# Bias rows sent out head by head beside the second mixer, constants loaded in two parts, and the first mixer's output projection done with split weights

## What is computed

```
def first_block(x, ...):
    ...
    for layer in range(DEPTH):                      # layer 0: even_mixer, layer 1: diff_mixer
        u = rms_norm(h, mix_norm_g[layer])
        h = h + mixer(u, ...)
        h = h + sq_relu_mlp(rms_norm(h, mlp_norm_g[layer]), mlp_w_up[layer], mlp_w_down[layer])
    return rms_norm(h, final_norm_g)
def even_mixer(h, w_in, cmp_pe, cmp_w1, cmp_w2, w_out, cos, sin):
    proj = jnp.einsum('btd,de->bte', h, w_in)
    ...
    o_a = dsa_attention(qa, ka, va, qi, ki, wi)     # 8 heads, top-k of an index score
    o_b = nsa_attention(qb, k_c, v_c, k_s, v_s, k_w, v_w, gb, cmp_pe, cmp_w1, cmp_w2)   # 8 heads
    o = jnp.concatenate([o_a.reshape(bsz, T, -1), o_b.reshape(bsz, T, -1)], axis=-1)
    return jnp.einsum('bte,ed->btd', o, w_out)
def moba_attention(h, w_qkv, w_o, rel_bias):        # the last mixer
    ...
        bias_own = rb[t5_bucket(jnp.maximum(dist_own, 0))].transpose(2, 0, 1)[None]
        logit_own = jnp.einsum('bhqd,bhkd->bhqk', qf, k_own.astype(jnp.float32)) * scale + bias_own
```

## Time and profile before

| | us |
|---|---|
| median of three runs (1263.09 to 1263.97) | 1263.24 |
| the profiled execution, as timed | 1265.12 |
| its span in the trace | 1263.2 |
| PE busy in the span | 1155.1 (91%) |
| DVE busy | 807.2 (64%) |
| ACT busy | 592.3 (47%) |

### The profile page before, as it was taken

How to read it: one execution, slowest core, us unless ns; L and a number is a source line. 1 busy time by engine, 2 the same in 40 slices (tenths; PEclk the granted TensorE clock), 3 DMA queues, 4 the chain that set the end, 5 groups by cost and what they waited for, 6 DMA issues and landing times.

```text
span 1263.2 us, 18055 instructions
## 1 busy us (share of the span) xinstructions
PE 1155.1 (91%) x7384; PEld 1015.3 (80%) x7384; DVE 807.2 (64%) x1287; ACT 592.3 (47%) x914; POOL 45.7 (4%) x88
## 2 busy tenths in 40 slices
PE   4169999999999999899999849999999998999997
PEld 4167675999998877699999649999978987999996
DVE  4035734787777666787777686877775556655554
ACT  5023534634445556564344545444446454644342
POOL 1010000000000000000000000000002000000000
PEclk9679999999999999999999969999999999999999
DMA  7852403797773433569777334977735434455530
GB/s 267 122 138 71 167 27 149 297 354 276 272 293 134 167 104 130 200 254 351 276 273 277 119 133 155 359 276 279 298 134 180 154 133 150 168 199 180 187 134 34
DMA packets 35810, 248.57 MB, mean 197 GB/s; under 512 B 4304, under 2 KB 4320, under 8 KB 6928
## 3 DMA queue, kind: packets, MB, share of 16 engines
q1 hardware_dynamic: 26352, 188.61, 40.3%
q0 software_dynamic: 9232, 57.69, 13.8%
q10 hardware_dynamic: 144, 1.12, 0.2%
HBM read 242.55 MB, written 4.19 MB: 195 GB/s over the span
## 4 chain that ended last, share of the span: by engine, by line
PE 80%; DVE 9%; ACT 4%; issue 4%; DMA 3%; POOL 0%; DVEq 0%; ACTq 0%; POOLq 0%
PE bank L1216 67%; DMA bias_rows<-PT 3%; PE bank L1398 2%; PE bank L1632 2%; PE bank L1423 1%; DVE wlo L700 1%; PE bank L1615 1%; ACT vo L426 1%; DVE x L720 1%; DVE wlo L811 1%; PE bank L1447 1%; PE bank L1446 1%; PE bank L1445 1%; DVE work L718 1%; PE bank L1696 1%
## 5 line engine op out<-in xcount | busy, mean ns | idle before, releaser
L700 DVE TENSOR_TENSOR wlo<-raw,whi 128x2048 fp32r<-128x2048 f32 (+2 forms) x143 | 324.6, 2274 | 138.0 <-ACT whi L416 137.9
L1216 PE MATMUL bank<-uh,whi 128*128 128x256 f32 x1272 | 369.6, 291 | 36.4 <-ACT vo L522 36.4
L1216 PE MATMUL bank<-ul,whi 128*128 128x256 f32 x1272 | 361.4, 284 | 0.0
L1216 PE MATMUL bank<-uh,wlo 128*128 128x256 f32 x1272 | 361.4, 284 | 0.0
L416 ACT ACTIVATE whi<-raw 128x2048 fp32r<-128x2048 f32 (+2 forms) x143 | 270.5, 1896 | 38.9 <-DMA bias_rows<-PT 37.8
L1216 PEld LDWEIGHTS bank<-uh,whi 128*128 128x128 f32 x1272 | 245.4, 193 | 44.8 <-issue 42.5
L1216 PEld LDWEIGHTS bank<-ul,whi 128*128 128x128 f32 x1272 | 245.5, 193 | 4.4 <-issue 2.2
L1216 PEld LDWEIGHTS bank<-uh,wlo 128*128 128x128 f32 x1272 | 245.2, 193 | 0.0
L1216 PE MATMUL bank<-whi,hh 128*128 128x512 f32 x544 | 214.0, 393 | 0.0
L1216 PE MATMUL bank<-wlo,hh 128*128 128x512 f32 x544 | 212.4, 390 | 0.0
L1216 PE MATMUL bank<-whi,hl 128*128 128x512 f32 x544 | 211.8, 389 | 0.0
(11 more groups left out here) (211 smaller groups left out, 1185.7 us busy)
## 6 DMA issues: line engine op xcount, KB each, us to landing
raw<-in_stream SPq DMA_DIRECT2D x176, 1024.0 KB, 4.9
qk<-in_w_mod POOLq DMA_DIRECT2D x48, 1024.0 KB, 5.9
bias_rows<-PT POOLq DMA_DIRECT2D x1, 3072.0 KB, 33.0
u<-bias_rows POOLq DMA_DIRECT2D x16, 128.0 KB, 2.7
raw<-in_stream SPq DMA_DIRECT2D x2, 696.0 KB, 12.5
con<-in_con ACTq DMA_DIRECT2D x1, 1098.5 KB, 6.9
x<-in_x SPq DMA_DIRECT2D x2, 512.0 KB, 8.1
vo<-in_fin_g POOLq DMA_DIRECT2D x2, 512.0 KB, 4.9
```

The costliest lines, as they stand in the source:

```text
L700: nc.vector.tensor_tensor(wlo[:, c % RING, 0:w], raw[:, raw_index(c) % RING, 0:w], whi[:, c % RING, 0:w].bitcast(fp32), ALU.subtract).then ...
L1216: ins = mm(out, st, mv, start=start and i == 0, stop=stop and i == 2, skip_group_check=True)
```

## The change

**Bias rows.** `gb` gets a buffer of its own, 16 by 384. ACT no longer waits for `bias_out`. POOL writes the rows in 16 DMAs, one for each head and so from one partition each, and head h waits until chunk h - 1 of DIFF is used. **Constants.** They are reordered: 337 columns that the start needs go first, on SP's queue behind the first half of x; the other 1860 go behind stream chunk 1, and DVE waits for them (`in_late`) ahead of the lower part of chunk 4. **Start.** ACT takes a square root of a constant before x is there, splits chunk 0 ahead of the gain of the first token tile and chunk 1 behind it, and DVE follows. **Projection back.** The four output chunks are split like the others (they get numbers 10 to 13, and MLP0 begins at 14). ACT writes the upper part of each attention output quarter and DVE the lower part, into `hh`/`hl` and `uh`/`ul`; PE uses `add_rows` (L1216 of before), three passes in place of one float32 product.

```
@@ sync @@
             for t in range(NT):
                 sp.dma_start(x[:, t, :], a["x"][128 * t:128 * t + 128, :]).then_inc(in_x[t], 16)
+                if t == 0:
+                    sp.dma_start(con[:, 0:C_EARLY], a["con"][:, 0:C_EARLY]).then_inc(in_con, 16)
             for n in range(NRAW):
+                if n == 2:
+                    sp.dma_start(con[:, C_EARLY:], a["con"][:, C_EARLY:]).then_inc(in_late, 16)
@@ gpsimd @@
-            pool.wait_ge(bias_sb, 1)
-            pool.dma_start(bass.AP(gdram.tensor, 0, [[128 * 512, 16], [512, 128], [1, 384]]),
-                           gb[:, :].unsqueeze(1).to_broadcast([16, 128, 384])).then_inc(bias_out, 16)
...
+                elif m == 1:
+                    for h in range(16):
+                        pool.wait_ge(used, DIFF + h)
+                        pool.dma_start(bass.AP(gdram.tensor, 128 * 512 * h, [[512, 1], [512, 128], [1, 384]]),
+                                       gb[h:h + 1, :].unsqueeze(1).to_broadcast([1, 128, 384])).then_inc(bias_out, 16)
@@ scalar @@
-            act.dma_start(con[:, :], a["con"]).then_inc(in_con, 16)
+            act.wait_ge(col_ready, 1)
+            nc.scalar.activation(std[:, 0:1], one, ACT.Sqrt)
             deviation(0)
-            hi_upto(1)
             act.wait_ge(in_con, 16)
             for t in range(NT):
+                hi_upto(t)
                 upper(0, t, vec[:, V_MIX:])
...
-            act.wait_ge(bias_out, 16)
...
-                    nc.scalar.activation(oT[c], bank[7 if c else 6][:, :].rearrange("p (b n) -> p b n", b=2), ACT.Copy)\
-                        .then_inc(e_oc, 1)
+                    nc.scalar.activation(out_part(c, True), bank[7 if c else 6][:, :].rearrange("p (b n) -> p b n", b=2), ACT.Copy)\
+                        .then_inc(e_oh, 1)
...
-                elif (i, q) in ((16, 0), (17, 0)):
-                    hi_upto(MLP0 + i - 16)
+                elif (i, q) in ((12, 3), (13, 2), (14, 2), (15, 1), (16, 1), (17, 1)):
+                    hi_upto(i - 2)
@@ vector @@
-            dve.wait_ge(in_con, 16)
             for t in range(NT):
                 scaled(0, t)
+            dve.wait_ge(in_con, 16)
...
-                elif (i, q) in ((16, 3), (17, 2)):
-                    lo_upto(MLP0 + i - 16)
+                elif (i, q) in ((13, 3), (14, 1), (14, 3), (15, 3), (16, 3), (17, 2)):
+                    lo_upto({(13, 3): 10, (14, 1): 11, (14, 3): 12, (15, 3): 13, (16, 3): 14, (17, 2): 15}[i, q])
+                if (i, q) in E_TURN_OUT:
+                    c = E_TURN_OUT[i, q]
+                    dve.wait_ge(e_oh, c + 1)
+                    nc.vector.tensor_tensor(out_part(c, False), bank[7 if c else 6][:, :].rearrange("p (b n) -> p b n", b=2),
+                                            out_part(c, True).bitcast(fp32), ALU.subtract).then_inc(e_ol, 1)
@@ tensor @@
                     if p in (8, 10):
-                        pe.wait_ge(e_oc, p // 2 - 2)
+                        pe.wait_ge(e_ol, p // 2 - 2)
...
-                even_back(c, even_steps(E_OUT + c))
+                pe.wait_ge(lo_ready, MLP0 - 4 + c + 1)
+                pe.wait_ge(e_ol, c + 1)
+                add_rows(MLP0 - 4 + c, 1, out_part(c, True), out_part(c, False), c == 0, c == 3, steps=steps)
```

More of the change, by code:

```diff
@@ L21 @@
 LAM_INIT = 0.8 - 0.6 * math.exp(-0.3)
-C_ID, C_SW, C_TRI = 0, 128, 256
-C_COS, C_SIN, C_COSQ, C_SINQ = 384, 640, 896, 1152
-C_CORR = 1408
+C_ID, C_VEC = 0, 128
+V_MIX, V_MLP, V_MIX2, V_MLP2, V_POOL, V_C, V_SUB = 0, 16, 32, 48, 64, 72, 80
+V_BMOD = 81
+V_PE = V_BMOD + 96
+C_EARLY = C_VEC + V_PE + 32
+C_SW = C_EARLY
+C_TRI = C_SW + 128
+C_COS, C_SIN, C_COSQ, C_SINQ = (C_TRI + 128 + 256 * i for i in range(4))
+C_CORR = C_SINQ + 256
 C_HB = C_CORR + 128
@@ L30 @@
 C_MASK = C_CMPN + NT * NBLK
-C_VEC = C_MASK + 384
-V_MIX, V_MLP, V_MIX2, V_MLP2, V_POOL, V_C, V_SUB = 0, 16, 32, 48, 64, 72, 80
-V_BMOD = 81
-V_PE = V_BMOD + 96
-C_END = C_VEC + V_PE + 32
+C_END = C_MASK + 384
 QA, QI, KA, KI, QB, KC, VC, KS, KW = 0, 4, 6, 7, 8, 12, 13, 14, 15
-EVEN, MLP0, DIFF, MLP1, POOL, MLP2, MOBA, MLP3, LAST = 0, 10, 42, 58, 90, 91, 123, 139, 171
+EVEN, MLP0, DIFF, MLP1, POOL, MLP2, MOBA, MLP3, LAST = 0, 14, 46, 62, 94, 95, 127, 143, 175
 MLPS = (MLP0, MLP1, MLP2, MLP3)
-NPLAIN = 8
-PLAIN_CMP, PLAIN_OUT = 8, 14
+NPLAIN = 4
+PLAIN_CMP = 8
 NRAW = LAST + NPLAIN
@@ L175, in build @@
         hT = sb("hT", [128, 2, 30])
+        gb = sb("gb", [16, 384])
         kcm = sb("kcm", [128, 30])
@@ L1617, in compress @@
                 ins.then_inc(plain_used, 1)
-            def even_back(c, steps):
-                n = PLAIN_OUT + c
-                pe.wait_ge(loaded[n % RING], loaded_value(n))
-                pe.wait_ge(e_oc, c + 1)
-                w = raw[:, n % RING, :].rearrange("p (k n) -> p k n", k=2)
-                for t in range(NT):
-                    for h in range(2):
-                        steps(2 * t + h)
-                        if c == 0:
-                            pe.wait_ge(*((e_add, 7), (vc_ready, 1), (e_add, 8), (e_oc, 1))[2 * t + h])
-                        for k in range(2):
-                            ins = mm(bank[acc_of(1)[2 * t + h]][:, :], oT[c][:, k, 128 * t:128 * t + 128],
-                                     w[:, k, 512 * h:512 * h + 512], start=c == 0 and k == 0, stop=c == 3 and k == 1,
-                                     skip_group_check=True)
-                        if c == 3 and (t, h) != (1, 1):
-                            ins.then_inc(acc_ready, 1)
-                ins.then_inc(plain_used, 1)
             pe.wait_ge(in_con, 16)
```

31 lines of the change are left out of this document (16 added, 15 removed).

## The result

| | before | changed |
|---|---|---|
| median (lowest to highest), us | 1263.61 (1263.09 to 1267.39, 4 runs) | 1224.79 (1221.87 to 1225.85, 4 runs) |
| profiled execution: timed / span, us | 1265.12 / 1263.2 | 1223.78 / 1222.0 |
| PE busy | 1155.1 | 1149.1 |

The ratio is 0.9683, with a 95% interval of 0.9657 to 0.9709: 3.2% faster, some 39 us by the medians and 41.2 by the two traces. The forecast was 1219.0 with a range of 1213 to 1243.

The account below looks back on a forecast made before the run. PE was 91% busy, so gains lay where it idled, chiefly from 37 to 71 us behind the bias-row DMA. Terms 35.3 + 2.0 + 4.85 + 2.1 = 44.2 off the median 1263.24 gave 1219.0 us, range 1213 to 1243.

Parts of the forecast that it names:

- The wait: Ahead of the first rotary swap: ACT no longer waits for the bias-row DMA, chunk 4's lower part starts 35.3 us earlier.
- The clock: Behind the first swap: PE's clock falls less once the long idle is gone; 2.0 us, between 1.1 and 2.8.
- The start: Up to PE's first product: chunk 0 lands earlier with fewer bytes ahead; 4.85 us, between 2.8 and 6.5.
- The projection back: End of the first mixer: three passes replace float32 products; 2.1 us gained after waits, between 0 and 4.3.
- The four waits: Projection back: PE waits 1.1, 1.1 and 0.9 us for DVE, then idles about 1.4 us ahead of the norm.
- the gain of a unit: Projection back: 0.39 us per unit, from 1.75 to 1.36; eleven units gain 4.3 us before waits.
- The heads: Second mixer: 16 bias-row DMAs at 2.06 us of all engines each fit beside the chunk loads; cost 0.
- Rival B: Second mixer: heads take 8.25 us each and hold the loads; price 10 to 35 us, middle 1241; chance 0.33.
- price rule: Second mixer: head plus load time on all engines counts against a chunk's time; 11.05 us against 7.9.
- D: Start and projection back give nothing or little, only the wait and clock gains come; 1227 us; chance 0.08.
- C: Second mixer: one partition sets the rate, a head takes 33 us; some 447 us more, 1666; chance 0.05.

Follow-up runs that it names:

- u_bias_early: The changed kernel with the bias rows sent in one 3 MB transfer straight behind the masked rows, from their own tile; 1248.43 us, ratio 0.984 to before.
- b_trial: The changed kernel with chunk 2's rotary step ahead of chunk 4's lower part, start loads reordered, ACT's and DVE's projection-back parts moved; 1218.57 us, one run.
- c_after: The changed kernel run again unaltered, beside the runs that undo parts of it; 1224.07 us, ratio 0.9661 to before.
- c_after_2: The changed kernel run again unaltered, on the same chip as the final faster version; 1225.73 us, ratio 0.9665 to before.
- m_bias_mid: The changed kernel with the bias rows sent in one 3 MB transfer in the first mixer, behind POOL's last key-row copy; 1237.16 us, one run.

## Why the prediction was right, term by term

**The wait: 35.3 forecast, 35.3 came.** The first swap was forecast near 36 (76.37 - 35.3 - 4.85 = 36.2) and came at 36.98; the 0.8 is the start's. What was late next was DVE's own list, as said. What the forecast did not see is that the wait also kept the copies of the key rows behind the transfer. With "removing a step from POOL's queue only lets its later steps go earlier" it passed over what the old place would have cost without the wait; u_bias_early showed 24 us. It didn't matter for this change, because both went together.

**The clock: 2.0 forecast, 1.0 came.** The mechanism was right, and the place too: 2.92 us of idle time ahead of the swap ("about 3"). The size is a draw between -0.3 and 2.5, and the forecast took a single value near the upper end; its lower bound of 1.1 was too high. Only the runs could tell that.

**The start: 4.85 forecast, 4.6 at the first product** (14.52 against 14.1), 4.1 at the masked rows; undone, it costs 4 to 6. Counting the bytes ahead of chunk 0 was right: 2.8 was counted, and its upper part starts 2.87 earlier. The 10.3 taken for the landing put another 0.5 on that which didn't come (the upper part starts at 10.70). From there to the first product it takes 3.82, and 3.8 was forecast.

**The projection back: 2.1 forecast, 1.3 came.** The four waits are there nearly as walked: 0.98 for 1.1, 0.84 for 1.1, 0.53 for 0.9, 1.37 for 1.4. The term that was mis-sized is the gain of a unit. The forecast had 0.39 for each of the eleven units ahead of the last ones, with 0.227 from one product to the next. Where a unit stands between other steps of PE its first product takes 0.31 to the next one, and the unit 1.47 in place of 1.77, so 0.3 or a little less. By the marks the eleven gained 1.30 + 0.98 + 0.84 = 3.1, or 0.28 each, in place of 4.3; the two waits took 1.8 in place of the 2.2. The third wait was rightly left out: it lies behind the last chunk's transposes, from which to the norm it takes 9.58 with the change as before. b_trial, with DVE's and ACT's parts moved, gained 1.4 more.

**The heads: 0 forecast, 0.3 or less came (the second mixer took 131.1, 131.0 and 130.8 in the three traces of the changed kernel, 130.8 before), for a wrong reason.** The term "at the old pace a head costs all engines 2.06 us" is off by a factor of 2.3: 4.8 were measured. Rival B had the mechanism, slow heads that hold the loads, and its price rule was shown by doubling the heads; its own size of a head, 8.25, was off the other way. Between the two lies the point that decides: the load's 2.4 and the head's 4.8 stay 0.9 under the chunk's 8.1. So this term was right by luck. The forecast's own sign for it, a bias DMA landing in 4 us or so, didn't come (9.4); of B's signs the busy engines nearly came (0.89 against 0.9 and more), the heads of 8 us and the waits of ACT for loads did not. B's chance of 0.33 was not too high.

**The other rivals.** D, no gain from start and back, asked for 1227, and the median of 1224.79 is nearer to that than to 1219. The marks decide: D wanted the first product after 17 and it came at 14.52, and undoing the start costs 4 to 6. C needed a head of 8.8 us of all engines or more, and it took 4.8.

The sum: 39.4 at the first swap and 1.0 behind it, 1.3 at the projection back make 41.7 at the residual; 41.2 are left at the end of the span, from 44.2 forecast. The medians are 38.8 apart, since before's is 1.5 below its profiled execution and the changed kernel's 1.0 above. Beside c_after and c_after_2 the kernel before had medians of 1266.21 and 1267.52, so there the gain is 42.1 and 41.8.

## What to carry to other kernels

When a wait for a long transfer is to go, look at what is issued behind that transfer on the same queue: the wait may have been hiding that these small copies are late anyway. Count a background transfer in engine time per step beside the loads' (here 4.8 + 2.4 of 8.1), not by whether it has time to land; doubling it on the chip shows in one run how near the edge it is. And of a transfer that repeats a small tile, spread the source over partitions before you look for a better place for it.

## What the hardware showed that was not expected

- One partition as source of 192 KB took 4.8 us of all 16 DMA engines in the mean of the stage (5.0 with the heads doubled, 6.3 for a head alone, at 26 GB/s), eight neighbours 1.4, eight partitions 16 apart 0.66. Sixteen neighbours in one transfer of 3 MB took 33.0 us, 2.06 for 192 KB, more of the engines' time than eight neighbours with a DMA of their own. Why, no run here separates.
- With the same program up to there and the same 2.92 us of idle time on PE the clock had a mean of 1.00, 0.79 or 0.65 from 37 to 45 us; with 0.72 or none it was 1.00 both times. This moves the total by up to 2.8 us.
- Small copies on a queue behind a 3 MB transfer landed after 34 us; loads on another queue at the same time after 25.2, where 4.8 is usual. The other queue is slowed down too, but not always to the end: in u_bias_early a load issued at 35.9 landed 12 us ahead of the transfer's end (71.4), in m_bias_mid the load issued at 81.8 landed only 0.7 ahead of it (104.8).
